# Two transformer blocks on one core: the cross attention's memory is normed, turned and half projected in block 1 and kept in HBM

## The reference

```python
def cross_attention(hn, mem_n, w_cq, w_ckv, w_co):
    q = (hn @ w_cq).reshape(B, S, X_HEADS, X_HEAD_DIM)
    k, v = jnp.split((mem_n @ w_ckv).reshape(B, M, 2, X_HEADS, X_HEAD_DIM), 2, axis=2)
    ...
    return o @ w_co

h = h + cross_attention(rmsnorm(h, norm_cross), rmsnorm(mem, norm_mem), w_cq, w_ckv, w_co)
```

## Time and profile before

| | |
|---|---|
| median of 3 runs | 2444.03 us (2443.91 to 2444.95) |
| profiled execution, its own time | 2446.64 us |
| span of the profiled execution | 2444.9 us |
| mean granted clock of TensorE | 0.952 |
| PE busy | 2153.3 us (88%) |
| DVE, ACT, POOL busy | 29%, 15%, 5% |
| moved by DMA | 528.05 MB, mean 216 GB/s |
| chain that ended last | PE 64%, DMA 26%, DVE 7% |

### The profile page before, as it was taken

How to read it: one execution, slowest core, us unless ns; L and a number is a source line. 1 busy time by engine, 2 the same in 40 slices (tenths; PEclk the granted TensorE clock), 3 DMA queues, 4 the chain that set the end, 5 groups by cost and what they waited for, 6 DMA issues and landing times.

```text
span 2444.9 us, 27087 instructions
## 1 busy us (share of the span) xinstructions
PE 2153.3 (88%) x11677; PEld 1064.6 (44%) x11677; DVE 710.4 (29%) x1770; ACT 357.6 (15%) x684; POOL 126.3 (5%) x157
## 2 busy tenths in 40 slices
PE   7999999969877878799999999999999698877775
PEld 3455444444333333355666754445554343333332
DVE  3235561251000000403778554021022510000004
ACT  3101220010000000202322442100021100000001
POOL 4000000000000000001000100000000000000000
PEclk9999999979999999899998999999999699999998
DMA  7212102449999999921100202152332499999996
GB/s 265 91 35 74 64 35 103 181 175 399 427 427 427 427 427 427 327 84 26 28 3 2 71 1 72 49 206 81 126 138 78 144 401 427 426 427 426 427 427 259
DMA packets 94156, 528.05 MB, mean 216 GB/s; under 512 B 13025, under 2 KB 27542, under 8 KB 66891
## 3 DMA queue, kind: packets, MB, share of 16 engines
q1 hardware_dynamic: 80160, 492.34, 49.8%
q0 software_dynamic: 10032, 21.22, 2.4%
q10 hardware_dynamic: 3834, 12.64, 1.4%
HBM read 514.02 MB, written 28.31 MB: 222 GB/s over the span
## 4 chain that ended last, share of the span: by engine, by line
PE 64%; DMA 26%; DVE 7%; issue 1%; ACT 1%; ACTq 0%; DVEq 0%; POOLq 0%; SPq 0%
PE ps L198 61%; DMA RING<-in_w 8%; DMA SC<-in_w_e_down 4%; DMA SC<-in_w 3%; DMA RING<-in_w_e_gate 3%; DMA RING<-in_w_e_up 3%; DMA XT<-in_w 1%; DMA XT<-in_w_e_down 1%; DMA SC<-in_w_e_gate 1%; DMA SC<-in_w_e_up 1%; DVE X L1780 1%; PE ps L363 1%; DVE X L1759 0%; PE ps L1385 0%; PE ps L2740 0%
## 5 line engine op out<-in xcount | busy, mean ns | idle before, releaser
L198 PE MATMUL ps<-SC 64*64 64x64 f32 (+5 forms) x5904 | 716.6, 329 | 98.5 <-DMA RING<-in_w_e_up 19.8
L198 PE MATMUL ps<-RING,SC 128*64 128x512 f32 (+2 forms) x1872 | 678.5, 612 | 74.5 <-DMA RING<-in_w_e_gate 21.6
L198 PE MATMUL ps<-XT,RING 128*128 128x512 f32 x1104 | 494.7, 601 | 6.3 <-DVE SC L2071 3.5
L198 PEld LDWEIGHTS ps<-SC 64*64 64x64 f32 (+3 forms) x5904 | 346.5, 145 | 344.0 <-issue 304.8
L198 PEld LDWEIGHTS ps<-RING,SC 128*64 128x64 f32 (+2 forms) x1872 | 240.2, 157 | 371.4 <-issue 367.9
L198 PEld LDWEIGHTS ps<-XT,RING 128*128 128x128 f32 x1104 | 208.2, 192 | 255.9 <-issue 248.6
L1549 DVE TENSOR_TENSOR SC<-SC,ps 128x512 f32<-128x512 f32 x32 | 22.0, 687 | 691.3 <-PE ps L198 691.3
L198 PE MATMUL ps<-XT,SC 128*64 128x512 f32 x352 | 162.1, 614 | 19.2 <-DMA SC<-in_w 9.9
L198 PE MATMUL ps<-RING,XT 128*128 128x512 f32 (+2 forms) x448 | 157.0, 504 | 0.0
L198 PE MATMUL ps<-SC,RING 128*128 128x512 f32 (+2 forms) x448 | 117.3, 429 | 0.1
L198 PEld LDWEIGHTS ps<-RING,XT 128*128 128x128 f32 x448 | 76.8, 197 | 73.6 <-issue 73.2
(11 more groups left out here) (404 smaller groups left out, 1469.5 us busy)
## 6 DMA issues: line engine op xcount, KB each, us to landing
RING<-in_w SPq DMA_DIRECT2D x41, 2048.0 KB, 33.8
SC<-in_w SPq DMA_DIRECT2D x41, 2048.0 KB, 33.7
RING<-in_w_e_gate SPq DMA_DIRECT2D x22, 2048.0 KB, 33.1
SC<-in_w_e_down SPq DMA_DIRECT2D x17, 2048.0 KB, 32.5
RING<-in_w_in SPq DMA_DIRECT2D x16, 2048.0 KB, 8.0
SC<-in_w_e_up SPq DMA_DIRECT2D x15, 2048.0 KB, 33.8
XT<-in_w SPq DMA_DIRECT2D x10, 2048.0 KB, 32.7
SC<-in_w_e_gate SPq DMA_DIRECT2D x10, 2048.0 KB, 34.4
```

Of the source, the lines that this page charges most:

```text
L198: return e.matmul(out, l, r, start=st, stop=sp, skip_group_check=True)
```

## The change

Block 1's plan gets the piece `me` (now with banks 4 to 7), between the last of `dh` and the output projection of `g1`: the memory is loaded into SC 10 and 11, normed, and turned in two halves into four tiles that are free then (rw_W, rw_B, KI and LR). ACT writes the turned memory to HBM (`memT`, 1 MB). The weights of the first half of the keys (`ck0`, 2 MB) are loaded into slot 8 (XT) by `mk_s`, as third load of the first mixture, and the rotation becomes (3, 0, 4, 7, 1, 2, 5, 6, 8). `mk_p` makes the first four of eight key tiles in three places of the first mixture's PE program: ahead of `cum` (8 calls), between `cum` and `idx` (12 calls), and after `idx` ahead of the first turn (12 calls). `mk_a` copies them out, and ACT writes them to HBM (`keysT`, 0.5 MB). In `mix2` the piece `me` is gone; `cr` reads both back from HBM at the place in the plan where `me` had begun, and computes only the second half of the keys. The load `ck0` is gone from `mix2`, so each later load of `mix2` takes the slot before its old one. The second mixture's rotation stays.

```diff
+    memT = nc.dram_tensor("memT", [128, 4, 512], F, kind="Internal").ap()
+    keysT = nc.dram_tensor("keysT", [128, 1024], F, kind="Internal").ap()
...
+    ME = Flow(book, "me", (4, 5, 6, 7))
+    me_X, me_N = scv(10, 2), scv(11, 2)
...
+    me_K = SC[:, 6, 1024:2048]
+
+    def me_p(e):
+        yield
+        yield
+        yield from half_turns(turn_p, e)
+        yield
+        yield
...
+    def me_a(e):
+        W.wait_ge(*DH.on("ev", "y", 2))
+        W.wait_ge(*DH.on("ev", "y", 3))
+        e.dma_start(me_X, t["mem_2"][0].rearrange("(t p) n -> p t n", p=128)).then_inc(*ME.up("dmem", "mem"))
+        yield
+        norm_a(e, me)
+        yield
+        yield from half_turns(turn_a, e)
+        yield
...
+        for n in range(4):
+            e.dma_start(memT[:, n, :], me_homes[n]).then_inc(*ME.up("dmt", "memT"))
+        yield
...
+    def mk_s(e):
+
+        s, free = slots.put(8, "ck0", (ME, ("k", 3)))
+        for f in free:
+            W.wait_ge(*f)
+        e.dma_start(s.rearrange("p (k n) -> p k n", k=8), t["w_ckv_2"][0].rearrange("(k p) n -> p k n", p=128)[:, :, 0:512]).then_inc(*slots.up("ck0"))
+
+    def mk_p(e, gap):
+
+        for n, k0, k1 in (((0, 0, 8),), ((1, 0, 8), (2, 0, 4)), ((2, 4, 8), (3, 0, 8)))[gap]:
...
+            for k in range(k0, k1):
+                i = mm(e, b[:, 0:256], w8("ck0")[:, k, n * 128:(n + 1) * 128], me.dst[:, k, :], k == 0, k == 7)
...
+    def mk_a(e, gap):
+        for n in ((0, 1, 2), (3,))[gap]:
+            W.wait_ge(*ME.on("k", n))
+            copy_a(e, me_K[:, 256 * n:256 * n + 256], ME.at("k", n)[:, 0:256]).then_inc(*ME.up("a", "ev", "k", n))
...
         def p(e):
+            pause["p"](e, 0)
             b, free = c.take("cum")
...
+            pause["p"](e, 1)
             b, free = c.take("idx")
...
+            pause["p"](e, 2)
             turn_e(e, c, 0, c.take)
...
         def a(e):
             idle(e)
+            pause["a"](e, 0)
             W.wait_ge(*c.on("ged"))
...
-    M0, moe0, (RT0, route0) = moe(0, G1_FLOWS, G1, [(G1, ("mix", 7))], ((3, 0, 8, 4, 7, 1, 2, 5, 6), {
-        8: [(G1, ("w", "g1b"))],        4: [(DH, ("ev", "y", 2)), (DH, ("ev", "y", 3))], 7: [(G1, ("mix", 7))], 5: [(G1, ("w", "wo0")), (G1, ("w", "wo1"))]}), lambda e: mix2_first(e))
+    M0, moe0, (RT0, route0) = moe(0, G1_FLOWS, G1, [(G1, ("mix", 7))], ((3, 0, 4, 7, 1, 2, 5, 6, 8), {
+        8: [(G1, ("w", "g1b"))],        4: [(ME, ("xt", 7))], 7: [(G1, ("mix", 7))], 5: [(G1, ("w", "wo0")), (G1, ("w", "wo1"))]}), lambda e: mix2_first(e), {"s": mk_s, "p": mk_p, "a": mk_a})
...
         for n, w in (("ck", "w_ckv_2"), ("cv", "w_ckv_2"), ("cq", "w_cq_2"), ("co", "w_co_2")):
-            for half in range(2):
+            for half in range(n == "ck", 2):
...
     def cr_p(e):
         c = CR
-        xt_ready(e, ME)
-        for half in range(2):
+        yield
+        W.wait_ge(*CR.on("mem"))
+        for half in range(1, 2):
...
     def cr_a(e):
         c = CR
+        W.wait_ge(*TL.on("ya", 3))
+        W.wait_ge(*ME.on("memT"))
+        W.wait_ge(*ME.on("keysT"))
+        e.dma_start(SC[:, 1, :], memT.rearrange("p a n -> p (a n)")).then_inc(*c.up("dmem"))
+        e.dma_start(SC[:, 2, 0:1024], keysT).then_inc(*c.up("dmem", "mem"))
+        yield
```

More of the change, by code:

```diff
@@ L354, in norm_v, with turn_p @@
             e.tensor_scalar(m.xn[:, i, :], m.src[:, i, :], m.R.y[:, i:i + 1], None, A.mult).then_inc(*c.up("v", "xn", i))
-    def turn_p(e, m):
+    def turn_p(e, m, ks=range(8)):
         c = m.c
-        for k in range(8):
+        for k in ks:
             b, free = c.take("xt", k)
@@ L1222, in mix1_s, with __init__, __getitem__ @@
         wload(e, "wo1", t["w_out"][0], 512, 512, (G1, ("w", "wo1")))
-    def moe(bi, before, out, clear, first, ahead=None):
+    class Parts:
+        def __init__(self, views):
+            self.views = views
+        def __getitem__(self, i):
+            return self.views[i[1]][i[0], i[2]]
+    ME = Flow(book, "me", (4, 5, 6, 7))
+    me_X, me_N = scv(10, 2), scv(11, 2)
+    me_homes = [rw_W[:, :, :].rearrange("p c j -> p (c j)")[:, 0:512], rw_B[:, :, :].rearrange("p c j -> p (c j)")[:, 0:512], KI[:, :], LR[:, :]]
@@ new lines, in me_v @@
+    def me_v(e):
+        yield
+        norm_v(e, me)
+        yield
+        yield from half_turns(turn_v, e)
+        yield
+        yield
+    def mk_s(e):
[5 more added lines that the diff above has]
+        for n, k0, k1 in (((0, 0, 8),), ((1, 0, 8), (2, 0, 4)), ((2, 4, 8), (3, 0, 8)))[gap]:
+            if k0 == 0:
+                W.wait_ge(*slots.on("ck0"))
+                xt_ready(e, ME)
+                b, free = ME.take_at(6 + n % 2, "k", n)
+                W.wait_ge(*free)
+            b = ME.at("k", n)
+            for k in range(k0, k1):
+                i = mm(e, b[:, 0:256], w8("ck0")[:, k, n * 128:(n + 1) * 128], me.dst[:, k, :], k == 0, k == 7)
+            if k1 == 8:
+                i.then_inc(*ME.up("p", "k", n))
@@ new lines, in mk_a, with moe @@
+    def mk_a(e, gap):
+        for n in ((0, 1, 2), (3,))[gap]:
+            W.wait_ge(*ME.on("k", n))
+            copy_a(e, me_K[:, 256 * n:256 * n + 256], ME.at("k", n)[:, 0:256]).then_inc(*ME.up("a", "ev", "k", n))
+        if gap:
+            for n in range(4):
+                W.wait_ge(*ME.on("ev", "k", n))
+            e.dma_start(keysT, me_K).then_inc(*ME.up("dkt", "keysT"))
+    def moe(bi, before, out, clear, first, ahead=None, pause=None):
+        pause = pause or {eng: lambda *a: None for eng in "spa"}
@@ L1315, in s @@
             while put_n < 6 * NPAIR:
+                if put_n == 2:
+                    pause["s"](e)
                 if put_n == len(first[0]):
@@ L1503, in down_a @@
                 e.activation(YS[:, q % 2, 0:512], at("down", q, 0)[:, :], AF.Copy).then_inc(*f.up("a", "ev", "down", q, 0))
+            if f is c and q == 1 and bi == 0:
+                W.wait_ge(*ME.on("keysT"))
             W.wait_ge(*f.on("down", q, 1))
@@ L1515, in a @@
             e.activation(v2, v2, AF.Exp).then_inc(*c.up("a", "ev2"))
+            pause["a"](e, 1)
             for q in range(NPAIR):
@@ L3001, in cr_a @@
         c = CR
+        W.wait_ge(*TL.on("ya", 3))
+        W.wait_ge(*ME.on("memT"))
+        W.wait_ge(*ME.on("keysT"))
+        e.dma_start(SC[:, 1, :], memT.rearrange("p a n -> p (a n)")).then_inc(*c.up("dmem"))
+        e.dma_start(SC[:, 2, 0:1024], keysT).then_inc(*c.up("dmem", "mem"))
+        yield
         norm_a(e, cr)
-        W.wait_ge(*TL.on("ya", 3))
-        for half in range(2):
+        for half in range(1, 2):
             for j in (0, 2):
```

41 lines of the change are left out of this document (15 added, 26 removed), and 6 rows, old and new, of the table PLANS.

## The result

| | before | after |
|---|---|---|
| median | 2444.2 us (2443.91 to 2444.95, 4 runs) | 2425.39 us (2424.76 to 2426.09, 4 runs) |
| profiled execution, its own time | 2446.64 us | 2425.11 us |
| span | 2444.9 us | 2423.4 us |
| mean granted clock | 0.952 | 0.955 |

The ratio is 0.9923, with a 95% interval of 0.9905 to 0.9940: 18.8 us faster by the medians.

The account below looks back on a forecast made before the run. In the mixtures the load stream and its start bind, elsewhere PE's chain. Terms +1.9 - 1.9 - 13.9 - 2.2 + 1.0 = -15.1 us took 2444.0 to 2428.9 us; range 2425.5 to 2436.0 us, 80%.

Parts of the forecast that it names:

- the two terms: First routing's calls (-2.2 us, bounds -3.9 and +0.9) and second mixture's late loads (+1.0 us); bounds together -17.8 to -10.5 us.
- Part 1: Memory's norm and turning moved from mix2 to g1: +1.9 us ahead of first mixture, -1.9 us in mix2, 0 together.
- Part 2: Cross attention: 32 calls, half of the keys, leave PE's chain there, -13.9 us taken whole.
- Part 3: First routing: calls fit PE's three waits and hold the clock up, -2.2 us, bounds -3.9 and +0.9.
- the signs that I had named: Among them: PE busy with clock above 0.8 between 521 and 541 us; half of w loads issued 1 to 3 us earlier.
- the transfers bind, not PE: First mixture's stream start: PE could release it 4.2 us earlier, but slot 8's load and `keysT` allow only 3.9 us.
- the -3.9 us: First routing, if the clock stays up throughout by the skill's rule taken strictly: end at 2427.2 us.
- Part 4: First loads of block 2: `wl` moves 7.8 us later, landing at 1031.1 us, needed at 1039.12 us; cost 0.
- Part 5: Second mixture: second load and four behind it wait for the output projection and may delay the first gather, +1.0 us.
- The leftover of transfers: Second mixture: some 2.4 us of late loads still left over when the first gather is issued at 1942.71 us.
- the sum: Whole kernel: +1.9 - 1.9 - 13.9 - 2.2 + 1.0 = -15.1 us, all counted in the profiled execution.

Follow-up runs that it names:

- experiment 2: Kernel before with only the memory's norm and turning moved to block 1, all keys left in the cross attention and the old first rotation: 2443.79 us.
- experiment 7: Kernel before with the three PE waits of its first routing filled by 9, 13 and 10 unused matmuls: 2439.38 us.
- experiment 4: Kernel before with only the second mixture's rotation altered, so its second load and the four behind wait for the output projection: 2445.11 us.
- experiments 8 and 12: Changed kernel with second routing's three waits filled: 2423.89 us; that plus calls split 8, 16, 8, six filling matmuls in first routing, old second rotation: 2421.39 us.
- experiment 10: Kernel before with four matmuls, whose results are overwritten, filling PE's 2.02 us wait ahead of g2's output projection: 2440.84 us.
- experiments 13 to 16: Only the memory's norm and turning moved, again; then kernel before with 8, 16, 24 more transposes in mix2: 2444.95, 2446.1, 2441.84, 2439.8 us, one run each.
- the repeat: The changed kernel again, unaltered, with a second profile: 2426.48 us.
- experiments 5 and 7: Changed kernel with calls split 8, 16 and 8: 2429.56 us; kernel before with its first routing's three waits filled by unused matmuls: 2439.38 us.

## Why the prediction was wrong by 3.7 us

The gain was 18.8 us and not 15.1; the time itself is 3.5 us below the forecast, since the median of the kernel before moved from 2444.0 to 2444.2 us. (The upper bounds of the two terms add up to -10.6 us, not -10.5; nothing hangs on it.)

**Part 1** (+1.9 and -1.9): right for the turning itself, +1.9 in g1 by ten profiles against eight. The 2443.79 us with part 1 alone hide two shifted falls of the clock that nearly cancel (experiment 2).

**Part 2** (-13.9): right, by 0.432 us a call with 28 of them left out, 13.8 us for 32.

**Part 3** (-2.2): right in size, -1.8 by the marks, and its clock prices were right (experiment 7). Its reason was not, and two of the signs that I had named failed: the clock was 0.76 in the mean from 521 to 541 us, not above 0.8, and half of w came 0.4 us earlier, not 1 to 3. I wrote that "the transfers bind, not PE", by slot 8's load and `keysT`. But the half of w loads go out with PE's half product (547.29 to 550.98 us), and the turn ahead of it waits for the last call, not for the gather. The calls ahead of `cum` were not hidden, those behind `idx` without any margin: a fall at 521 us, which I had not expected, and one at 538 us, which I had, ate the rest of the gain. The rule of the Trainium skill cited there (TensorE: Matmul & The Clock Gate, "What's actually happening"), that activity releases the throttle, agrees with experiment 7: with all three waits filled its windows have a clock of 1.00 from 528 us on. Taken as strictly as I did for the -3.9 us, it does not describe the changed kernel, whose clock was 0.51 in 7.00 us in which PE was never idle.

**Part 4** (0): right, with more room than forecast. `wl`'s last load went out at 1018.98 us, 2.4 us later than before and not 7.8, it landed 6.1 us behind that, and `lx` began at 1039.12 us, as before.

**Part 5** (+1.0): +1.3 by the marks and +1.2 by experiment 4, neither to be told from nothing. Its mechanism is worth less than that: in the changed kernel the gather took 4.53 us to the turn, 0.3 more than before, so that the agreement of +1.3 with the forecast is in part luck. The leftover of transfers that I reckoned at 2.4 us costs 1.9 us once PE is quick (experiments 8 and 12). The rule of the Trainium skill cited there (DMA: Bandwidth & Descriptors, "Issuing engines are not separate DMA queues"), by which transfers of all issuers interleave, held: by it the gather is not free of the loads.

**The step that failed is the sum**, which took every stretch outside the routings as unaltered. Its term -1.9 in mix2 measured -3.0 us, and its term -13.9 measured -15.5 us for its stretch, though 32 calls are only 13.8. The 1.7 us that the calls don't explain are one fall of the clock at g2's output projection. In the kernel before it came in all four profiles with the wait unfilled and the work ahead of it as it was, in the changed kernel in none of eight. Filling the wait took it away (experiment 10), and so did shifting the wait by 1.9 and 2.85 us, while 0.95 us left it. With part 1 alone, all calls of the keys still in place, it was missing in both profiles. So this part of the gain is shown, and it comes with the shift of the work ahead, against the beat of the clock (experiments 13 to 16), not with the saved calls. The changed kernel's wait is also shorter, 1.67 us and not 2.02, and what that adds was not tested. The shorter wait is 0.35 of the 1.1 us that -3.0 has over -1.9. With the wait of 2.02 us, DVE's last step ahead of the projection waits 2.37 us for PE's products, in the changed kernel 2.02. Why is open.

The other 0.7 to 0.8 us of the 1.1 I put down to fewer falls. The missing clock (time times the share not granted) from `lx` to g2's projection adds up to 17.4 us in the mean of the five profiles of the kernel before and its like in that row of the table (15.4 to 20.5), and to 16.4 us in the eight of the changed kernel (13.7 to 17.1). That is argued from the profiles, and their spread is wider than the difference.

The last 1.6 us between the marks' 17.2 and the medians' 18.8 us stay open; the repeat gave 17.4 us. Single runs of the kernel before spread over 10 us, and my range reached only 3.4 us below the forecast, with no room for falls outside the routings.

## What to carry to other kernels

Work that is moved into TensorE's waits can gain twice, by its own time and by what it does to the clock behind it, and the second gain wants the wait filled nearly to its end: the same 32 calls cost 12 to 13 us more in one place than spread over three, and four of them taken from the last place put off the next stage by 1.9 us in the one profile of that split, which filling the wait gave back. Before a difference of 2 us is explained by a change, lay the same marks into several profiles of both kernels: here one wait of 2 us cost 1.7 us or nothing, and a shift of one to two microseconds in the work ahead decided. A transfer that is "early enough" should be held against the gather of a faster engine, not against today's.

## What the runs showed of the hardware

- A wait of 2.02 us of PE at one place of the program was followed by a window with a clock of 0.5 to 0.7 in five profiles and of 1.00 in four (the starts stand with experiments 13 to 16); each fall made the stretch behind it 1.7 us longer. Falls begin on a beat that is even within an execution and whose offset differs between executions; the wait's place against it separates the five from the four. The Trainium skill (TensorE: Matmul & The Clock Gate, "What's actually happening") says that the gate's watch runs freely and isn't reset when a kernel starts. These rows agree; it is the part of that section that I had not used.
- A fall can also come with no long wait just ahead: in the changed kernel the clock was 0.51 in 521 to 528 us, with PE busy throughout, behind two waits of 0.79 and 0.78 us, and again 0.57 in 538 to 542 us behind one of 1.46 us.
- With 1.9 or 2.85 us of transposes added to PE's chain a run was no slower (2441.84 and 2439.8 against 2446.78 us). These are single runs, within the spread of the kernel before, so no gain is shown.
- A 2 MB load that was issued 2.2 us behind a gather (541.99 against 539.77 us) stood beside a gather that took 4.94 us to the turn instead of 4.05 (experiments 5 and 7). Whether the load did it was not tested.
- Starting the second stream up to 5 us earlier (1933.48 against 1938.40 us) left its length alone (451.58 against 451.19 us, and 452.23 in the second profile of the changed kernel). In these profiles the time moves with the stream's start.
